# Two expert layers in a transformer kernel: where the output is multiplied by its gate row

## The chip, the cores and the metric

The kernel runs on one core of one Trainium2 chip. A core has four compute engines that matter here, each with its own instruction queue: TensorE (PE, matrix products into the accumulation memory PSUM), VectorE (DVE), ScalarE (ACT) and GpSimd (POOL). SyncE (SP) issues the transfers from device memory (DMA). The engines wait for each other through semaphores. The metric is the device time of one execution, in microseconds (us), as a median of several runs.

## The reference, cut to what matters

256 tokens of width 1024 pass through two layers (an attention or retention mixer, then an expert layer) and then through a third block that the change doesn't touch. The expert layer is:

```python
def grouped_moe(h, ...):
    combine = ...        # two experts per token, both from the token's one group of four
    for e in range(N_EXPERTS):                                # 16 experts, 4 groups
        hidden = jax.nn.silu(t @ w_gate[e]) * (t @ w_up[e])
        out = out + combine[:, e:e + 1] * (hidden @ w_down[e])
    return out

y = grouped_moe(h, ...)
x = layer_norm(DEEPNORM_ALPHA * x + (1.0 + gate) * y, ln_g[i, 1], ln_b[i, 1])
```

`gate` is one row of 1024 numbers, the same for all tokens, so the product with (1 + gate) is one by column: it may be taken before or after the tokens are put back in their places.

## The kernel before, in words

`moe_stage` is one expert layer; it runs twice (names moe0 and moe1). Tokens are sorted by their group into 128 slots per group with 0/1 matrices (`hot`), and each group's slots pass its four experts. A branch picks this "gathered" form, or a dense one when a group has more than 128 tokens.

The weights come as a stream of 2 MB chunks, three per expert (gate, up, down), 48 per layer, into a ring of three buffers. SP fetches a chunk into a buffer when `chunk_used` says that the buffer's last chunk is done with. Products are made in split precision: each chunk is worked in four quarters (q = 0 to 3, 128x1024 each). ACT copies a quarter to its high part `w_hi` (line 1115), DVE subtracts that from the quarter to get the low part `w_lo` (line 1191), and PE takes three products with them: high by high, high by low, low by high (lines 1029 to 1031 for the gate and up chunks, line 1048 for the down chunks). There is one buffer for each of the four quarters, so that ACT may write quarter q of the next chunk only when PE is done with quarter q of this one (`q_used`), and PE may start quarter q when DVE has made its low part (`lo_done`). DVE releases the chunk after its fourth quarter.

The down products of a group's four experts add up in PSUM banks 6 and 7, a tile of 128 slots x 1024. When the last is done, the sum is taken out, split in the same manner: ACT copies it to `y_hi` (`take`, line 1138), then DVE subtracts that from PSUM to get `y_lo`, a view of `halves` (`take_low`, line 1207). In the loop over groups (three turns per layer, one for each of groups 0 to 2) this stands among the next expert's gate chunk: on ACT between its quarters 1 and 2, on DVE between its quarters 2 and 3. PE waits for `y_low` only before the next down product. The last group's sum is taken out behind all weights. The order on each engine is the order of the code; there is no scheduler.

Then PE scatters the slots back to tokens (`scatter`, line 1089, `hotT` by `y_hi` and `y_lo`, four groups) into banks 0 to 3: two tiles of 128 tokens (tt), two halves of 512 columns (dh). It does groups 0 to 2 of tt = 0 first (12 products), waits for the last `y_low`, then does group 3 of tt = 0 (two products for each half) and all of tt = 1. `norm.y_made` counts the four finished quarter tiles. DVE turns each into the normalised output (`LayerNorm.vector_half`, lines 449, 451, 452): times the gate row, plus ALPHA times x, statistics. The gate row lies in `K.mod[:, 2 * D:3 * D]`; it is made during the first group's experts (`GateRow`, semaphore `gate.taken`). `LayerNorm` is shared with the two mixers.

In the second layer the norm ends with a product with rows g and b (lines 1498 and 1500) that SP fetches late (lines 483 and 484), then a second norm and transposes.

Of the kernel before, what the change touches and what calls it, by code (L numbers as in the profile page):

```python
# [401 lines left out]
class LayerNorm:  # L402

    def __init__(self, K, scope, name, s, split=False, last=False, by_half=False):
        self.K, self.s, self.split, self.last, self.by_half = K, s, split, last, by_half
        sb = lambda n, shape: scope.enter_context(K.nc.sbuf_tensor(f"{name}_norm_{n}", shape, F32))
# [38 lines left out]
    def vector_half(self, dve, n, tt, half):  # L445

        K, c, s, cols = self.K, self.c, self.s, slice(half * 512, (half + 1) * 512)
        dve.wait_ge(self.y_made, n + 1)
        c.do(dve.tensor_tensor(s[:, tt, cols], K.bank[:, 2 * (1 - half) + tt if self.by_half else 2 * tt + half, :], K.mod[:, 2 * D + half * 512:2 * D + (half + 1) * 512],
                               ALU.mult))  # L450
        c.do(dve.scalar_tensor_tensor(s[:, tt, cols], K.x[:, tt, cols], ALPHA, s[:, tt, cols], ALU.mult, ALU.add))
        c.do(dve.bn_stats(self.stats[:, tt, half, :], s[:, tt, cols]))
# [368 lines left out]
def moe_stage(K, layer):  # L821
# [15 lines left out]
    with ExitStack() as stage:  # L837
# [12 lines left out]
        g_row, b_row = K.mod[:, D:2 * D], sb("b_row", [P, D])[:]  # L850
        norm = LayerNorm(K, stage, name, room[:, 2 * D:4 * D].rearrange("p (t d) -> p t d", t=TT), split=(layer == 0), last=(layer == 1))
        gate = GateRow(K, name, 2 * layer + 1, 2)
# [97 lines left out]
        def combine(dve, c):  # L950
# [13 lines left out]

        made, spread_w, slot_taken, hot_ready, wide_ready, gathered, slots_h, slots_l, y_low = (
            s_(s) for s in ("made", "spread_w", "slot_taken", "hot_ready", "wide", "gathered", "slots_h", "slots_l", "y_low"))
        hi_done, lo_done, q_used, turned, hid_h, hid_l, taken = (
# [138 lines left out]
        def scalar_gathered(act):  # L1106
# [26 lines left out]

            def take(g, done):

                act.wait_ge(q_used, done)
                out = y_hi[:, g, :] if isinstance(g, int) else y_hi[:, bass.ds(g, 1), :].rearrange("p o d -> p (o d)")
                act.activation(out, K.bank[:, 6:8, :].rearrange("p b c -> p (b c)"), ACT.Copy).then_inc(taken, 1)
# [10 lines left out]
            def experts(i):  # L1149
                for r in range(PER_GROUP):  # L1150
# [5 lines left out]
                    elif r == 1 and i is not None:  # L1156
                        high(of(i, r, 0), {1: lambda: take(i, Q * 3 * PER_GROUP * i + Q * (3 * PER_GROUP + 3))})
                    elif r == 2 and i is None:
# [18 lines left out]
            high((LAST_DOWN, 0, None), {1: lambda: hidden_high(EXPERTS)})  # L1177
            take(GROUPS - 1, Q * (LAST_DOWN + 2))

        def vector_gathered(dve, c_):  # L1180
# [54 lines left out]
            def experts(i):  # L1235
                for r in range(PER_GROUP):
# [101 lines left out]
        def vector_dense(dve, c):  # L1338
# [24 lines left out]
            with dve.Fori(0, LOOPS) as i:  # L1363
                for r in range(2):
                    make_hidden(2 * i + (2 + r), r, 6 * i + (n0 + 7 + 3 * r))

        with nc.Block() as block:
# [2092 lines left out]
```

## Time and profile before

| | us |
|---|---|
| runs before: median of 3 (lowest, highest) | 2244.33 (2239.88, 2246.12) |
| the profiled execution, its device time | 2244.5 |
| its span, first to last instruction | 2242.8 |
| PE busy | 2077.7 (93%) |
| DVE busy | 1610.0 (72%) |
| ACT busy | 1131.2 (50%) |

All durations below come from the profiled execution. What lies around its span is 2244.5 - 2242.8 = 1.7 us. The expert layers' products by group run from about 240 to 525 us and from about 820 to 1105 us. In a view in order of time a row is an instruction or several merged; the number in brackets is the idle time of the engine before it, and after the arrow stands who ended it. A busy PE instruction is longer than the distance to the next, since they overlap: the distance counts.

### The profile page before, as it was taken

The page shows a single profiled execution, that of the slowest core. Times are in us where ns is not written, and L with a number is a line of the kernel's source. Part 1 is how long each engine was busy: PE and PEld are TensorE (multiplying, and loading weights), DVE is VectorE, ACT ScalarE, POOL GpSimd, SP SyncE. Part 2 cuts the span into 40 slices and gives each one's busy share as a digit, 9 for nine tenths or more (in the row PEclk, how much of TensorE's full clock was granted, in tenths as well). Part 3 has the DMA queues.
Part 4 walks back from the last instruction along what each step waited for, and adds up shares of the span by engine and source line. Part 5 has one row for each costly group of instructions (what it writes and reads, how often), then busy time and mean ns, then how long its engine had stood idle before and what let it go on. Part 6 is the DMA issues. An engine that isn't in the chain of part 4 may idle for free. (4 is left out here: it accounts for less than half of the span.)

```text
span 2242.8 us, 33580 instructions
## 1 busy us (share of the span) xinstructions
PE 2077.7 (93%) x11164; PEld 1720.3 (77%) x11164; DVE 1610.0 (72%) x2587; ACT 1131.2 (50%) x1641; POOL 693.7 (31%) x468
## 2 busy tenths in 40 slices
PE   5898999996999889999888999899899999999998
PEld 4775767775877776777676656899899999888887
DVE  4367888887367888888878651399779998555555
ACT  5352767774335376777550233355444444445454
POOL 6620040001757504000030004599967773000000
PEclk8997999998999989999989999999999999999999
DMA  9864789995457658899832333255444445555554
GB/s 394 310 219 148 298 305 354 343 347 193 178 201 294 246 189 322 339 347 343 306 100 75 111 109 146 88 174 174 163 136 145 141 140 180 193 188 191 191 189 150
DMA packets 76634, 485.70 MB, mean 217 GB/s; under 512 B 9472, under 2 KB 9984, under 8 KB 58624
## 3 DMA queue, kind: packets, MB, share of 16 engines
q1 hardware_dynamic: 75824, 482.88, 59.2%
q10 hardware_dynamic: 720, 1.61, 0.2%
q8 instruction: 57, 0.93, 0.2%
q14 instruction: 33, 0.27, 0.0%
HBM read 483.41 MB, written 1.05 MB: 216 GB/s over the span
## 5 line engine op out<-in xcount | busy, mean ns | idle before, releaser
L1191 DVE TENSOR_TENSOR moe_w_lo<-ring,moe_w_hi 128x1024 fp32r<-128x1024 f32 x384 | 467.1, 1252 | 52.1 <-ACT moe_w_hi L1115 38.3
L1115 ACT ACTIVATE moe_w_hi<-ring 128x1024 fp32r<-128x1024 f32 x376 | 385.1, 1058 | 75.0 <-PE bank L1048 43.2
L3083 POOL TENSOR_TENSOR peer_u_lo<-peer_u,peer_u_hi 128x512 fp32r<-128x512 f32 x253 | 343.3, 1368 | 97.0 <-ACT peer_u_hi L3108 95.0
L3023 PE MATMUL bank<-peer_hn_hi,peer_u_hi 128*128 128x256 f32 x1024 | 295.7, 289 | 17.9 <-POOL peer_u_lo L3083 11.9
L3024 PE MATMUL bank<-peer_hn_lo,peer_u_hi 128*128 128x256 f32 x1024 | 287.6, 281 | 0.0
L3025 PE MATMUL bank<-peer_hn_hi,peer_u_lo 128*128 128x256 f32 x1024 | 287.4, 281 | 0.0
L229 POOL TENSOR_TENSOR ret_all_w_lo<-ring,ret_all_w_hi 128x1024 fp32r<-128x1024 f32 x64 | 158.1, 2479 | 293.7 <-ACT ret_all_w_hi L219 293.1
L3108 ACT ACTIVATE peer_u_hi<-peer_u 128x512 fp32r<-128x512 f32 x253 | 159.2, 629 | 129.7 <-PE bank L3025 120.4
L1029 PE MATMUL bank<-moe_w_hi,moe_slots_hi 128*128 128x512 f32 x512 | 210.5, 411 | 11.7 <-DVE moe_w_lo L1191 7.7
L3023 PEld LDWEIGHTS bank<-peer_hn_hi,peer_u_hi 128*128 128x128 f32 x1024 | 194.7, 190 | 19.9 <-POOL peer_u_lo L3083 13.6
L1031 PE MATMUL bank<-moe_w_hi,moe_slots_lo 128*128 128x512 f32 x512 | 201.0, 393 | 0.0
L1030 PE MATMUL bank<-moe_w_lo,moe_slots_hi 128*128 128x512 f32 x512 | 200.6, 392 | 0.0
L3024 PEld LDWEIGHTS bank<-peer_hn_lo,peer_u_hi 128*128 128x128 f32 x1024 | 194.7, 190 | 0.0
L3025 PEld LDWEIGHTS bank<-peer_hn_hi,peer_u_lo 128*128 128x128 f32 x1024 | 194.2, 190 | 0.0
L3236 DVE TENSOR_TENSOR peer_v_lo<-peer_scores,peer_v_hi 128x1024 fp32r<-128x1024 f32 x86 | 105.4, 1225 | 102.0 <-ACT peer_v_hi L3128 102.0
L3128 ACT ACTIVATE peer_v_hi<-peer_scores 128x1024 fp32r<-128x1024 f32 x86 | 91.2, 1061 | 118.7 <-PE bank L3063 112.0
L1029 PEld LDWEIGHTS bank<-moe_w_hi,moe_slots_hi 128*128 128x128 f32 x512 | 96.0, 188 | 57.5 <-DVE moe_w_lo L1191 38.9
L3216 DVE TENSOR_SCALAR peer_scores<-consts,peer_selT 128x128 f32<-128x128 f32 x256 | 131.2, 572 | 0.0
L3063 PE MATMUL bank<-peer_hn_hi,peer_hn_lo 128*128 128x512 f32 x504 | 121.4, 390 | 0.0
L219 ACT ACTIVATE ret_all_w_hi<-ring 128x1024 fp32r<-128x1024 f32 x64 | 67.3, 1058 | 105.0 <-PE bank L258 76.4
L329 DVE CUSTOM_DVE_ANT_0 mod<-sb_mod_ring,bank 128x1024 bf16<-128x1024 f32 x64 | 77.1, 1218 | 58.6 <-DMA sb_mod_ring<-in_ada_t 40.6
L1031 PEld LDWEIGHTS bank<-moe_w_hi,moe_slots_lo 128*128 128x128 f32 x512 | 96.1, 188 | 21.8
(517 smaller groups left out, 4570.4 us busy)
## 6 DMA issues: line engine op xcount, KB each, us to landing
ring<-in_stream SPq DMA_DIRECT2D x135, 2048.0 KB, 8.3
peer_u<-in_peer_u SPq DMA_DIRECT2D x128, 512.0 KB, 3.2
peer_scores<-in_peer_v SPq DMA_DIRECT2D x86, 512.0 KB, 4.3
sb_mod_ring<-in_ada_t SPq DMA_DIRECT2D x64, 512.0 KB, 6.4
peer_u<-in_peer_v SPq DMA_DIRECT2D x42, 512.0 KB, 4.3
ret_mod_ring<-in_ada_t SPq DMA_DIRECT2D x32, 512.0 KB, 5.0
s_bz<-in_b_channel SPq DMA_DIRECT2D x4, 512.0 KB, 5.8
ring<-in_stream SPq DMA_DIRECT2D x2, 1024.0 KB, 5.0
```

The lines of the kernel that those rows point to most:

```text
L229: pool.tensor_tensor(self.shaped(self.w_lo, q, by_columns), self.quarter(n, q, by_columns), self.shaped(self.w_hi, q, by_columns).bitcast( ...
L1029: pe.matmul(K.bank[:, m, :], x_high, high[:, cols], start=(k == 0), stop=False)
L1030: pe.matmul(K.bank[:, m, :], x_high, low[:, cols], start=False, stop=False)
L1031: last = pe.matmul(K.bank[:, m, :], x_low, high[:, cols], start=False, stop=(k == KD - 1))
L1115: act.activation(w_hi[:, q, :], K.ring[:, at % RING, q * CHUNK // Q:(q + 1) * CHUNK // Q], ACT.Copy).then_inc(hi_done, 1)
L1191: dve.tensor_tensor(w_lo[:, q, :], K.ring[:, at % RING, q * CHUNK // Q:(q + 1) * CHUNK // Q], w_hi[:, q, :].bitcast(F32), ALU.subtract).th ...
L3023: pe.matmul(out, u_hi[:, b, k2, :], h_hi[:, k, :], start=(k == 0), stop=False)
L3024: pe.matmul(out, u_hi[:, b, k2, :], h_lo[:, k, :], start=False, stop=False)
L3025: last = pe.matmul(out, u_lo[:, b, k2, :], h_hi[:, k, :], start=False, stop=(k == KD - 1))
L3083: pool.tensor_tensor(u_lo[:, b, :, :], u[:, i, KD // 2 * half:KD // 2 * (half + 1), :], u_hi[:, b, :, :].bitcast(F32), ALU.subtract).then_ ...
L3108: act.activation(u_hi[:, b, :, :], u[:, i, KD // 2 * half:KD // 2 * (half + 1), :], ACT.Copy).then_inc(hi_made, 1)
L3216: last = dve.tensor_scalar(a_hot[:, b, q, :], K.iota, selT[:, 0, one], selT[:, 1, one], ALU.is_equal, ALU.mult)
```

## The change

The product with the gate row is moved from behind the scatter to in front of the split. In the two expert layers `vector_half` no longer does line 449: its first instruction is now the one with ALPHA, which reads PSUM itself. In its place DVE multiplies each group's sum in PSUM banks 6 and 7 by the row, in place (`gate_y`), and ACT's `take` waits for that (`y_gated`) and no longer for PE's last quarter. The mixers' norms stay as they were. The dense form gets the product too, at its end.

```diff
@@ class LayerNorm, vector_half
         dve.wait_ge(self.y_made, n + 1)
-        c.do(dve.tensor_tensor(s[:, tt, cols], K.bank[:, ...], K.mod[:, 2 * D + half * 512:2 * D + (half + 1) * 512],
-                               ALU.mult))
-        c.do(dve.scalar_tensor_tensor(s[:, tt, cols], K.x[:, tt, cols], ALPHA, s[:, tt, cols], ALU.mult, ALU.add))
+        y = K.bank[:, ...]
+        if not self.gated:
+            c.do(dve.tensor_tensor(s[:, tt, cols], y, K.mod[:, 2 * D + half * 512:2 * D + (half + 1) * 512], ALU.mult))
+            y = s[:, tt, cols]
+        c.do(dve.scalar_tensor_tensor(s[:, tt, cols], K.x[:, tt, cols], ALPHA, y, ALU.mult, ALU.add))
         c.do(dve.bn_stats(self.stats[:, tt, half, :], s[:, tt, cols]))
@@ moe_stage, ACT
-            def take(g, done):
-                act.wait_ge(q_used, done)
+            def take(g):
+                act.wait_ge(y_gated, g + 1)
@@ moe_stage, DVE
+            gate_row = K.mod[:, 2 * D:3 * D]
+            def gate_y(done):
+                dve.wait_ge(gate.taken, 2)
+                dve.wait_ge(q_used, done)
+                y = K.bank[:, 6:8, :].rearrange("p b c -> p (b c)")
+                dve.tensor_tensor(y, y, gate_row, ALU.mult).then_inc(y_gated, 1)
@@ in the loop over groups, DVE
-                        low(chunk(i, r, 0), {2: lambda: take_low(i)})
+                        low(chunk(i, r, 0), {0: lambda: gate_y(Q * 3 * PER_GROUP * i + Q * (3 * PER_GROUP + 3)), 2: lambda: take_low(i)})
@@ behind all weights, DVE
             low((LAST_DOWN, 0), {1: lambda: hidden_low(EXPERTS)})
+            gate_y(Q * (LAST_DOWN + 2))
             take_low(GROUPS - 1)
```

On DVE, in the loop over groups, at the gate chunk that follows a group's last down product. Before (`moe_w_lo<-ring` are the quarters' low parts, `halves<-bank` is `take_low`):

```order
L1191 TENSOR_TENSOR moe_w_lo<-ring,moe_w_hi 128x1024 [waits moe0_hi]
L1190 REGISTER_ALU
L1191 TENSOR_TENSOR moe_w_lo<-ring,moe_w_hi 128x1024 [waits moe0_hi]
L1190 REGISTER_ALU
L1191 TENSOR_TENSOR moe_w_lo<-ring,moe_w_hi 128x1024 [waits moe0_hi]
L1204 REGISTER_ALU
L1207 ISA [waits moe0_taken]
L1207 TENSOR_TENSOR halves<-bank,moe_y_hi 128x1024
L1190 REGISTER_ALU
L1191 TENSOR_TENSOR moe_w_lo<-ring,moe_w_hi 128x1024 [waits moe0_hi]
```

The same place now:

```order
L1193 TENSOR_TENSOR moe_w_lo<-ring,moe_w_hi 128x1024 [waits moe0_hi]
L1209 ISA [waits moe0_gate_taken]
L1211 TENSOR_TENSOR bank<-bank,mod 128x1024 [waits moe0_q_used]
L1192 REGISTER_ALU
L1193 TENSOR_TENSOR moe_w_lo<-ring,moe_w_hi 128x1024 [waits moe0_hi]
L1192 REGISTER_ALU
L1193 TENSOR_TENSOR moe_w_lo<-ring,moe_w_hi 128x1024 [waits moe0_hi]
L1214 REGISTER_ALU
L1217 ISA [waits moe0_taken]
L1217 TENSOR_TENSOR halves<-bank,moe_y_hi 128x1024
L1192 REGISTER_ALU
L1193 TENSOR_TENSOR moe_w_lo<-ring,moe_w_hi 128x1024 [waits moe0_hi]
```

One 128x1024 product from PSUM to PSUM stands between quarter 0 and quarter 1; quarters 1 to 3 and `take_low` are behind it.

On DVE behind the first layer's scatter, the first two quarter tiles. Before:

```order
L449 TENSOR_TENSOR moe_room<-bank,mod 128x512 [waits moe0_gate_taken,moe0_norm_y_made,moe0_x_made,moe0_norm_dve]
L451 SCALAR_TENSOR_TENSOR moe_room<-x,moe_room 128x512 [waits moe0_norm_dve]
L452 BN_STATS moe_norm_stats<-moe_room 128x6 [waits moe0_norm_dve]
L449 TENSOR_TENSOR moe_room<-bank,mod 128x512 [waits moe0_norm_y_made,moe0_norm_dve]
L451 SCALAR_TENSOR_TENSOR moe_room<-x,moe_room 128x512 [waits moe0_norm_dve]
L452 BN_STATS moe_norm_stats<-moe_room 128x6 [waits moe0_norm_dve]
L455 BN_AGGR moe_norm_mv<-moe_norm_stats 128x2 [waits moe0_norm_dve]
```

Now:

```order
L453 SCALAR_TENSOR_TENSOR moe_room<-x,bank 128x512 [waits moe0_gate_taken,moe0_norm_y_made,moe0_x_made,moe0_norm_dve]
L454 BN_STATS moe_norm_stats<-moe_room 128x6 [waits moe0_norm_dve]
L453 SCALAR_TENSOR_TENSOR moe_room<-x,bank 128x512 [waits moe0_norm_y_made,moe0_norm_dve]
L454 BN_STATS moe_norm_stats<-moe_room 128x6 [waits moe0_norm_dve]
L457 BN_AGGR moe_norm_mv<-moe_norm_stats 128x2 [waits moe0_norm_dve]
```

Two instructions for a quarter tile are left of three.

## Rows read from the trace of the kernel before

**Rows 1.** The page: the span.

```profile
span 2242.8 us, 33580 instructions
```

**Rows 2.** Windows, two turns of the group loop: stretch, length, engines' busy time, clock, DMA share, GB/s.

```profile
303.57:376.41 72.84, 70.49 (x301) 53.22 (x300) 64.26 (x58) 53.61 (x57) 9.15 (x6) 1.00 0.90 338
376.41:449.20 72.79, 70.68 (x306) 54.25 (x305) 62.95 (x58) 53.36 (x57) 0.00 (x0) 1.00 0.91 346
```

**Rows 3.** Waits, 252 to 525 us: who for whom, total us, times, longest.

```profile
ACT moe_w_hi L1115 <- DMA ring<-in_stream: 4.7, 4, 1.6
...
PE bank L1029 <- DVE moe_w_lo L1191: 3.9, 6, 0.7
```

**Rows 4.** In order of time, DVE around a group's take: start, length, what.

```profile
388.12 2.36 DVE L1191 TENSOR_TENSOR moe_w_lo<-ring,moe_w_hi 128x1024 fp32r<-128x1024 f32 x2 [0.22 <-ACT moe_w_hi L1115]
391.98 1.23 DVE L1191 TENSOR_TENSOR moe_w_lo<-ring,moe_w_hi 128x1024 fp32r<-128x1024 f32 x1 [1.51 <-ACT moe_w_hi L1115]
393.13 1.22 DVE L1207 TENSOR_TENSOR halves<-bank,moe_y_hi 128x1024 f32 x1
394.26 1.22 DVE L1191 TENSOR_TENSOR moe_w_lo<-ring,moe_w_hi 128x1024 fp32r<-128x1024 f32 x1
```

**Rows 5.** In order of time, ACT at the same place.

```profile
389.98 1.03 ACT L1138 ACTIVATE moe_y_hi<-bank 128x1024 f32 x1 [1.93 <-PE bank L1048]
390.91 3.88 ACT L1115 ACTIVATE moe_w_hi<-ring 128x1024 fp32r<-128x1024 f32 x4
```

**Rows 6.** In order of time, PE there: quarters 0, 1, 2, 3 begin.

```profile
389.69 0.39 PE L1029 MATMUL bank<-moe_w_hi,moe_slots_hi 128*128 128x512 f32 x1
...
391.05 0.39 PE L1029 MATMUL bank<-moe_w_hi,moe_slots_hi 128*128 128x512 f32 x1
...
393.26 0.50 PE L1029 MATMUL bank<-moe_w_hi,moe_slots_hi 128*128 128x512 f32 x1 [0.70 <-DVE moe_w_lo L1191]
...
395.53 0.50 PE L1029 MATMUL bank<-moe_w_hi,moe_slots_hi 128*128 128x512 f32 x1 [0.59 <-DVE moe_w_lo L1191]
```

**Rows 7.** One line: line 1207, all eight, minimum, median and maximum ns.

```profile
L1207 DVE TENSOR_TENSOR halves<-bank,moe_y_hi x8: 1217/1218/1226, 320.3 to 1106.5; 128x1024 f32 x6, 128x1024 fp32r<-128x1024 f32 x2
```

**Rows 8.** One line: ACT copies from PSUM into PSUM and into SBUF, ns.

```profile
L3101 ACT ACTIVATE bank<-bank x65: 368/368/368, 1646.7 to 1882.6; 128x256 f32<-128x256 f32 x65
L3101 ACT ACTIVATE H<-bank x63: 383/385/388, 1446.7 to 1636.6; 128x256 f32 x60, 128x256 f32<-128x256 f32 x3
```

**Rows 9.** In order of time, first layer's end: ACT, then PE, then DVE.

```profile
525.17 1.02 ACT L1138 ACTIVATE moe_y_hi<-bank 128x1024 fp32r<-128x1024 f32 x1 [4.65 <-PE bank L1048]
...
527.73 0.40 PE L1089 MATMUL bank<-moe_y_hi,moe_hotT 128*128 128x512 f32 x1
...
526.23 1.22 DVE L1207 TENSOR_TENSOR halves<-bank,moe_y_hi 128x1024 fp32r<-128x1024 f32 x1 [4.27 <-ACT moe_y_hi L1138]
...
527.86 0.17 DVE L339 TENSOR_TENSOR cols<-cols,mods 128x8 f32<-128x8 f32 x1
528.49 0.69 DVE L449 TENSOR_TENSOR moe_room<-bank,mod 128x512 f32<-128x512 f32 x1 [0.47 <-PE bank L1089]
529.22 0.69 DVE L451 SCALAR_TENSOR_TENSOR moe_room<-x,moe_room 128x512 f32<-128x512 f32 x1
```

**Rows 10.** In order of time, second layer's end: DVE, then SP.

```profile
1108.78 0.69 DVE L449 TENSOR_TENSOR moe_room<-bank,mod 128x512 f32<-128x512 f32 x1 [1.03 <-PE bank L1089]
...
1117.70 0.12 DVE L1497 RECIPROCAL moe_norm_std<-moe_norm_std 128x1 f32<-128x1 f32 x1
...
1103.63 1.04 SPq L484 DMA_DIRECT2D moe_b_row<-in_ln_b  x1
```

**Rows 11.** One line: line 484 between 1100 and 1110 us, issue to landing.

```profile
DMA to landing us min/median/max: 11.9/11.9/11.9
```

**Rows 12.** Windows, columns as in rows 2: before the first layer's end, and the stretch after it.

```profile
515.00:525.00 10.00, 8.59 (x41) 6.88 (x40) 6.02 (x6) 3.24 (x4) 0.00 (x0) 1.00 0.93 341
...
547.00:556.00 9.00, 3.37 (x16) 3.37 (x17) 4.52 (x6) 5.18 (x5) 5.78 (x3) 0.51 0.58 207
```

More of the change, by code:

```diff
@@ L402, with __init__ @@
 class LayerNorm:
-    def __init__(self, K, scope, name, s, split=False, last=False, by_half=False):
-        self.K, self.s, self.split, self.last, self.by_half = K, s, split, last, by_half
+    def __init__(self, K, scope, name, s, split=False, last=False, by_half=False, gated=False):
+        self.K, self.s, self.split, self.last, self.by_half, self.gated = K, s, split, last, by_half, gated
         sb = lambda n, shape: scope.enter_context(K.nc.sbuf_tensor(f"{name}_norm_{n}", shape, F32))
@@ L448, in vector_half @@
         dve.wait_ge(self.y_made, n + 1)
-        c.do(dve.tensor_tensor(s[:, tt, cols], K.bank[:, 2 * (1 - half) + tt if self.by_half else 2 * tt + half, :], K.mod[:, 2 * D + half * 512:2 * D + (half + 1) * 512],
-                               ALU.mult))
-        c.do(dve.scalar_tensor_tensor(s[:, tt, cols], K.x[:, tt, cols], ALPHA, s[:, tt, cols], ALU.mult, ALU.add))
+        y = K.bank[:, 2 * (1 - half) + tt if self.by_half else 2 * tt + half, :]
+        if not self.gated:
+            c.do(dve.tensor_tensor(s[:, tt, cols], y, K.mod[:, 2 * D + half * 512:2 * D + (half + 1) * 512], ALU.mult))
+            y = s[:, tt, cols]
+        c.do(dve.scalar_tensor_tensor(s[:, tt, cols], K.x[:, tt, cols], ALPHA, y, ALU.mult, ALU.add))
         c.do(dve.bn_stats(self.stats[:, tt, half, :], s[:, tt, cols]))
@@ L850, in moe_stage @@
         g_row, b_row = K.mod[:, D:2 * D], sb("b_row", [P, D])[:]
-        norm = LayerNorm(K, stage, name, room[:, 2 * D:4 * D].rearrange("p (t d) -> p t d", t=TT), split=(layer == 0), last=(layer == 1))
+        norm = LayerNorm(K, stage, name, room[:, 2 * D:4 * D].rearrange("p (t d) -> p t d", t=TT), split=(layer == 0), last=(layer == 1), gated=True)
         gate = GateRow(K, name, 2 * layer + 1, 2)
@@ L957, in combine @@
             dve.sem_inc(weights_ready, 1)
-        made, spread_w, slot_taken, hot_ready, wide_ready, gathered, slots_h, slots_l, y_low = (
-            s_(s) for s in ("made", "spread_w", "slot_taken", "hot_ready", "wide", "gathered", "slots_h", "slots_l", "y_low"))
+        made, spread_w, slot_taken, hot_ready, wide_ready, gathered, slots_h, slots_l, y_gated, y_low = (
+            s_(s) for s in ("made", "spread_w", "slot_taken", "hot_ready", "wide", "gathered", "slots_h", "slots_l", "y_gated", "y_low"))
         hi_done, lo_done, q_used, turned, hid_h, hid_l, taken = (
@@ L1156, in experts @@
                     elif r == 1 and i is not None:
-                        high(of(i, r, 0), {1: lambda: take(i, Q * 3 * PER_GROUP * i + Q * (3 * PER_GROUP + 3))})
+                        high(of(i, r, 0), {1: lambda: take(i)})
                     elif r == 2 and i is None:
@@ L1177, in scalar_gathered @@
             high((LAST_DOWN, 0, None), {1: lambda: hidden_high(EXPERTS)})
-            take(GROUPS - 1, Q * (LAST_DOWN + 2))
+            take(GROUPS - 1)
         def vector_gathered(dve, c_):
@@ L1365, in vector_dense @@
                     make_hidden(2 * i + (2 + r), r, 6 * i + (n0 + 7 + 3 * r))
+            dve.wait_ge(gate.taken, 2)
+            dve.wait_ge(norm.y_made, 2 * TT)
+            for tt in range(TT):
+                y = K.bank[:, 2 * tt:2 * tt + 2, :].rearrange("p b c -> p (b c)")
+                c.do(dve.tensor_tensor(y, y, K.mod[:, 2 * D:3 * D], ALU.mult))
         with nc.Block() as block:
```

## The prediction

> **What bounds the kernel now.** I read the two expert layers alone, since nothing else is edited, inside a span of 2242.8 us [rows 1]. First the windows: two turns of the group loop take 72.84 and 72.79 us, PE is busy for 70.49 and 70.68 of them, DVE for 64.26 and 62.95, ACT for 53, and the DMA share is 0.90 [rows 2]. PE bounds the loop, and DVE is close behind it. The waits then say what keeps PE from being quite full: it waits for DVE's low parts, and ACT waits for weights only 4 times in 273 us, 4.7 us together [rows 3]. A delay of PE in this loop is therefore not taken back by a transfer that would have been late anyway.
>
> The order of time around a group's take shows where PE waits. The chain there is serial over two engines. ACT takes the sum at 389.98, which it had waited for (1.93 us), and makes the high part of quarter 2 only then, from 390.91 [rows 5]. DVE had made quarters 0 and 1 from 388.12, idled 1.51 us, made low part 2 at 391.98, `take_low` at 393.13, low part 3 at 394.26 [rows 4]. PE begins its quarters at 389.69, 391.05, 393.26 and 395.53, and idles 0.70 and 0.59 before the last two [rows 6]. So `take`, high part 2, low part 2, `take_low`, low part 3, quarter 3 is a chain without slack that ends on PE. Whatever starts `take` later moves PE's quarter 3 by the same amount.
>
> At a layer's end PE is done with the weights, and the bound passes from PE to DVE: from 528.49 DVE works through the quarter tiles nearly without a gap, one instruction each 0.73 us (528.49 to 529.22) [rows 9].
>
> **Part 1: the product in the loop, six times.** DVE does low part 0 (388.12 and some 1.2 us, done at 389.35) and then stands before `gate_y` until PE has finished the down products, which is what ACT waited for until 389.98. Queued behind this wait are low parts 1 to 3 and `take_low`. The price of the product itself no row shows, as no DVE instruction of this trace writes PSUM. The nearest row is line 1207, which reads the same PSUM tile and an SBUF tile of the same size: 1218 ns at the median of eight [rows 7]. On ACT a copy from PSUM into PSUM takes 368 ns and one into SBUF 385 [rows 8], so a PSUM target has no price there. I take 1.22. The lower bound is the same row, since the elements are as many; the upper one is twice it, 2.44, if reading and writing PSUM took turns.
>
> `gate_y` then ends at 389.98 + 1.22 = 391.20. From DVE to the next engine a wait takes 0.05 us (low part 2 ends at 393.21, PE starts at 393.26) [rows 4, 6], so `take` starts at 391.25, 1.27 late. High part 2, low part 2, `take_low` and low part 3 follow at their old distances, and PE's quarter 3 goes from 395.53 to 396.80: +1.27. Low part 1 lies elsewhere: DVE starts it 1.14 behind `gate_y`, at 391.12, it is done at 392.35, and PE starts quarter 1 at 392.40 in place of 391.05. That is a new wait of 1.35 us on PE, but it isn't added: quarter 1 takes some 1.4 us, PE is free at 393.8, and low part 2 lets it go on at 394.53 only, which is the old 393.26 + 1.27. DVE's old idle time of 1.51 us is used up by the product, and that is the cover it has; the cover on the chain through ACT is none.
>
> From quarter 3 on all engines are late by the same 1.27, the release of the chunk and so the next fetch too. So nothing downstream changes its spacing, and nothing pays back: PE is busy for 97% of the turn. 3 turns in 2 layers: 6 x 1.27 = **+7.6 us**.
>
> **Part 2: the layer's end, twice.** ACT's take at 525.17 becomes `gate_y`; it, `take` and `take_low` stand in a row, so `take_low`, which ended at 526.23 + 1.22 = 527.45, ends 1.27 later, at 528.72. PE meanwhile scatters groups 0 to 2 until 527.73 [rows 9], 0.28 us beyond the old end: of the 1.27 the scatter hides 0.28 less the 0.05 of the wait, and group 3 starts at 528.77, 1.04 late. DVE's first quarter tile goes from 528.49 to 529.53. The small instructions of `norm_columns` (the last at 527.86 [rows 9]) shift behind `take_low` and end before that. The second layer has the same places (first tile at 1108.78 after a wait of 1.03 [rows 10]): +1.04 as well.
>
> **Part 3: the four products taken away, in each layer.** Each is one step of DVE's chain, 0.73 us [rows 9]: 4 x 0.73 = 2.9 us. PE feeds this chain early enough, also when 1.04 late: eight products of 0.23 for each later quarter tile, while DVE needs 1.45 for a tile and does statistics and transposes between. The new first instruction reads PSUM where it read SBUF; line 449 with its PSUM source and line 451 from SBUF both take 0.69 [rows 9], so I add nothing. Net of a layer's end: 1.04 - 2.92 = -1.88, twice **-3.8 us**.
>
> The page on the VectorE of the Trainium skill speaks against this last zero ("VectorE: DVE Perf Modes", section "The TRN2 errata — SBUF-src ops pay a fixed extra latency per instruction"): its table gives a PSUM source a fixed part of 120 cycles where SBUF has 58, so by an estimate from that page the instruction would grow by 0.065 us, eight times, +0.5 us in all, and the sum would be 2248.8. The trace has the two sources equal, 0.69 each, and I go by it.
>
> One cover is thin. In the second layer DVE needs row b before 1117.70 (line 1497 stands behind that wait); it is issued at 1103.63 and lands 11.9 us later, at 1115.5 [rows 10, 11]. The issue hangs on the weights and doesn't move against them, the need comes 1.88 earlier, at 1115.8. It still fits, by 0.3 us. Late by more, it would eat from the gain, at most 1.88 of it.
>
> **The sum.** 2244.5 + 7.6 - 3.8 = **2248.3 us**, 3.8 above the profiled execution, which is 0.2 above the median of the runs. It is +0.2%. A measurement of this kernel tells about 0.3% from no change, so the bounds of "the same" are 2237.6 and 2251.1.
>
> **Rivals.**
> 1. *The loop hides the product.* DVE idles 1.51 us just there [rows 4], more than the 1.22 it costs, and the DMA share of 0.90 could make the transfers the true bound, which would then not feel a late PE. Against it: the idle time lies behind `take`, not beside it, and transfers were waited for 4 times only [rows 3]. Then only the ends count: 2244.5 - 3.8 = 2240.7. Chance 0.10.
> 2. *PSUM to PSUM takes turns.* 2.44 us for the product, so 1.22 more at eight places, all on a chain: 2248.3 + 9.8 = 2258.1, slower. It decides from (2251.1 - 2248.3) / 8 = 0.35 us above my price, at 1.57 for one product. ACT's rows speak against it [rows 8]. Chance 0.08.
> 3. *The ring loses its slack.* A chunk released late is fetched late, and transfers that ran beside each other before might no longer. If each turn waited once more for weights by the mean of those seen, 4.7 / 4 = 1.2 [rows 3], that is 6 x 1.2 = 7.2 more: 2255.5, slower. Against it: release and need move together. Chance 0.12.
> 4. *The clock.* PE's new wait of 1.35 us stands in the loop. Before the first layer's end a window with 1.41 us of idle PE has a granted clock of 1.00 (2.4 GHz), and behind the layer it is 0.51 (1.2 GHz) with PE busy for 3.37 us [rows 12]. The first says that the loop keeps its clock. The second says that the next stage begins at the low level, and where the level changes may now fall otherwise against the work: half of 3.37 either way, twice, 2244.9 to 2251.7. Chance 0.10.
>
> That the change doesn't do what it says needs the dense form to run; line 1207 belongs to the other form and ran eight times [rows 7], so I give that nothing.
>
> **The numbers.** My forecast has 0.60; its own spread is some 3 us, as the runs before lie 6 apart. Within 0.3%: 0.50 of the forecast, 0.08 of rival 1, 0.02 of rival 3, 0.08 of rival 4: 0.68. Slower: 0.10, all of rival 2, 0.10 and 0.01: 0.29. Faster: 0.03. The range goes from 2240.0, just below rival 1, to 2254.5, most of the way to rival 3; outside lie rival 2, half of rival 3 and the tails, some 0.2.
>
> **What would show it.** Eight rows of the product at 1.2 us each; anything above 1.57 is rival 2. Turns of the loop of 74.1 us in place of 72.8 (72.8 again: rival 1; 75 and more with longer waits of ACT for the ring: rival 3). In a turn, PE waits three times behind the take, the first time for 1.3 us at quarter 1. From the layer's last weight product to the last instruction of the norm 1.9 us less, twice. The forecast is wrong if the turn grows by something other than 1.27, or if the ends give less than 3.8 since row b comes late.

## The result and the profile after

The changed kernel takes 2248.6 us, the median of 20 runs (2246.87 to 2252.94); the kernel before, run beside it on the same chips, takes 2244.3 (20 runs, 2239.88 to 2246.85). The ratio is 1.0023, 95% interval 1.0017 to 1.0030: slower by 4.3 us. Forecast were 2248.3 us and +3.8. Of the chances given, "within 0.3%" came true. The profiled execution has a span of 2247.9 us, 5.1 above [rows 1].

The first rows to look for are those of the new instruction. One line of the trace of the changed kernel, with count, minimum, median and maximum in ns (it answers to rows 7):

```profile
L1211 DVE TENSOR_TENSOR bank<-bank,mod x8: 1231/1232/1233, 317.4 to 1114.5; 128x1024 f32<-128x1024 f32 x8
```

A product that reads a PSUM tile and writes it back costs 1.23 us, 14 ns more than the split's subtraction from the same tile into SBUF. Next the turns of the group loop, as windows of the changed kernel (columns as in rows 2), the two turns of the first layer:

```profile
318.80:392.94 74.14, 71.04 (x304) 54.15 (x304) 64.14 (x59) 53.38 (x58) 0.00 (x0) 1.00 0.90 340
392.94:466.92 73.98, 70.96 (x304) 54.14 (x304) 64.14 (x59) 53.49 (x57) 0.00 (x0) 1.00 0.90 341
```

A turn is here taken from one ACT take to the next; cut in the same way, the turns before are 72.86 and 72.77 us in the first layer and 72.85 and 72.84 in the second. After, they are 74.14, 73.98, 74.06 and 74.11: 1.25 us longer at the mean. PE's clock is 1.00 (2.4 GHz) in both and the DMA share 0.90 beside 0.90 and 0.91 [rows 2], so neither explains it. The order of time around a group's take does. DVE of the changed kernel, then ACT, then PE (start, length, engine, what, and in brackets the wait ahead of it), where rows 4, 5 and 6 stand for before:

```profile
389.79 1.23 DVE L1193 TENSOR_TENSOR moe_w_lo<-ring,moe_w_hi 128x1024 fp32r<-128x1024 f32 x1 [0.23 <-ACT moe_w_hi L1117]
391.58 1.23 DVE L1211 TENSOR_TENSOR bank<-bank,mod 128x1024 f32<-128x1024 f32 x1 [0.56 <-PE bank L1050]
392.72 1.22 DVE L1193 TENSOR_TENSOR moe_w_lo<-ring,moe_w_hi 128x1024 fp32r<-128x1024 f32 x1
394.94 1.22 DVE L1193 TENSOR_TENSOR moe_w_lo<-ring,moe_w_hi 128x1024 fp32r<-128x1024 f32 x1 [1.00 <-ACT moe_w_hi L1117]
396.08 1.22 DVE L1217 TENSOR_TENSOR halves<-bank,moe_y_hi 128x1024 f32 x1
```

```profile
392.94 1.02 ACT L1140 ACTIVATE moe_y_hi<-bank 128x1024 f32 x1 [3.23 <-DVE bank L1211]
393.86 3.90 ACT L1117 ACTIVATE moe_w_hi<-ring 128x1024 fp32r<-128x1024 f32 x4
```

```profile
391.38 0.39 PE L1031 MATMUL bank<-moe_w_hi,moe_slots_hi 128*128 128x512 f32 x1
...
393.99 0.50 PE L1031 MATMUL bank<-moe_w_hi,moe_slots_hi 128*128 128x512 f32 x1 [1.09 <-DVE moe_w_lo L1193]
...
396.22 0.50 PE L1031 MATMUL bank<-moe_w_hi,moe_slots_hi 128*128 128x512 f32 x1 [0.57 <-DVE moe_w_lo L1193]
...
398.49 0.49 PE L1031 MATMUL bank<-moe_w_hi,moe_slots_hi 128*128 128x512 f32 x1 [0.61 <-DVE moe_w_lo L1193]
```

ACT now waits for the product (3.23 us in place of 1.93) and takes the sum 1.36 after the product began. PE's four quarters begin at 391.38, 393.99, 396.22 and 398.49. From quarter 0 to quarter 3 that is 7.11 us, where it was 5.84 [rows 6]: +1.27. It has three waits where it had two; the new one, 1.09 at quarter 1, widens the first step from 1.36 to 2.61, and quarter 2 then waits no longer than before.

The other half of the change is at a layer's end. The first layer of the changed kernel in order of time, DVE, ACT and PE (answers to rows 9):

```profile
529.41 1.23 DVE L1211 TENSOR_TENSOR bank<-bank,mod 128x1024 f32<-128x1024 f32 x1 [3.29 <-PE bank L1050]
530.68 1.02 ACT L1140 ACTIVATE moe_y_hi<-bank 128x1024 fp32r<-128x1024 f32 x1 [6.00 <-DVE bank L1211]
531.74 1.23 DVE L1217 TENSOR_TENSOR halves<-bank,moe_y_hi 128x1024 fp32r<-128x1024 f32 x1 [1.09 <-ACT moe_y_hi L1140]
...
533.02 0.51 PE L1091 MATMUL bank<-moe_y_hi,moe_hotT 128*128 128x512 f32 x1 [0.97 <-DVE halves L1217]
...
533.90 0.69 DVE L453 SCALAR_TENSOR_TENSOR moe_room<-x,bank 128x512 f32<-128x512 f32 x1 [0.37 <-PE bank L1091]
534.63 0.69 DVE L454 BATCH_NORM_STATS2 moe_norm_stats<-moe_room 128x6 f32<-128x512 f32 x1
```

Product, take and low part stand in a row, PE waits 0.97 us for them ahead of group 3, and each quarter tile of the norm has one 0.69 us instruction where it had two. The one that is left, line 453, now reads PSUM and still takes 0.69.

**The account.** I cut both traces at three events of each layer: its first low part, the start of its scatter, and the end of DVE's last instruction of its norm. What is between the two layers' expert work I call the mixer stretch, and the rest is what comes before and behind. In us, the profiled executions:

| segment | before | after | difference | forecast |
|---|---|---|---|---|
| first layer, loop | 305.87 | 310.47 | +4.60 | +3.8 |
| first layer, end | 22.73 | 21.05 | -1.68 | -1.88 |
| mixer stretch | 251.3 | 253.4 | +2.2 | 0 |
| second layer, loop | 306.28 | 310.22 | +3.94 | +3.8 |
| second layer, end | 21.08 | 19.75 | -1.33 | -1.88 |
| start and rest | 1335.5 | 1333.0 | -2.6 | 0 |

The last line is -0.4 ahead of the first layer and -2.1 behind the second. The edited segments alone sum to +5.5. The 2.2 and the -2.1 that cancel lie in code that the change does not touch; the last part of the experiments is about them.

### The profile page after: what moved, and what is told of

The parts are those of the page before. It is cut to its first block and busy times, and to the rows that moved or that the text cites. A ratio compares the mean times of both kernels' runs of the same rounds, so it can differ in the third digit from the quotient of the medians.

```text
span 2247.9 us, 33588 instructions
## 1 busy us (share of the span) xinstructions
PE 2080.6 (93%) x11164; PEld 1720.6 (77%) x11164; DVE 1607.6 (72%) x2587; ACT 1131.4 (50%) x1641; POOL 694.1 (31%) x468
## 5 line engine op out<-in xcount | busy, mean ns | idle before, releaser
L3039 PE MATMUL bank<-peer_hn_hi,peer_u_hi 128*128 128x256 f32 x1024 | 295.4, 288 | 17.9 <-POOL peer_u_lo L3099 11.9
```

The lines of the kernel that those rows point to most:

```text
L3039: pe.matmul(out, u_hi[:, b, k2, :], h_hi[:, k, :], start=(k == 0), stop=False)
```

## The experiments

The questions: is it the chain through the take that makes the loop longer, as forecast, or DVE's added work or the transfers? Do the ends give what was priced? And, once the chain was found, can it be taken off? Each of these kernels was run beside before on the same chip, and its ratio is to that. A trace shows one execution of a kernel, a median several, so the two need not agree to the microsecond.

**One half of the change at a time.** `norm_only` leaves the product out at both places, and so out of both layers:

```
-                        low(chunk(i, r, 0), {0: lambda: gate_y(...), 2: lambda: take_low(i)})
+                        low(chunk(i, r, 0), {2: lambda: take_low(i)})
...
-            gate_y(Q * (LAST_DOWN + 2))
```

> This kernel leaves the product with the gate row out of both expert layers altogether: the four products per layer behind the scatter are gone and none stands in the loop or in front of the last split. It measures part 3 alone. By the forecast's term 8 x 0.73 = 5.8 us less than before, 2238.5. The rival, that the forecast came out right because two wrong terms cancelled (the ends give less, the loop costs less), expects 2240 to 2243 here, since a shorter norm would then meet another wait, such as PE's scatter or the late row b of the second layer.

Measured: 2237.4 us beside 2245.0, ratio 0.9965 (0.9951 to 0.9978), so -7.7 where -5.8 was expected. Its loop turns are as before (72.75, 72.75, 72.79, 72.78). Its first end is 2.94 us shorter than before, where 4 x 0.73 = 2.92 was forecast. Its second gives 1.58 only, and the order of time of DVE there says why:

```profile
1110.55 0.21 DVE L457 BATCH_NORM_AGGREGATE moe_norm_mv<-moe_norm_stats 128x2 f32<-128x12 f32 x1
1111.95 0.16 DVE L1512 RECIPROCAL moe_norm_std<-moe_norm_std 128x1 f32<-128x1 f32 x1 [1.20 <-DMA moe_b_row<-in_ln_b]
```

DVE waits 1.20 us for row b. This is the thin cover of the prediction's part 3: with the need 2.92 earlier in place of 1.88, it is gone. The two ends explain 4.5 us. The profiled execution is 7.3 shorter than before, and the other 2.7 are spread over all the other segments, none of them over 1.5 (mixer stretch -0.3, rest -1.5). What they are I can't say; the interval, 3 us to either side, also holds the 5.8 expected.

`loop_only` is the other half: the product in the loop for groups 0 to 2, and the norm's products kept as well, so that the gate row comes in twice for these groups. ACT takes the last group's sum as before.

```
-        norm = LayerNorm(..., last=(layer == 1), gated=True)
+        norm = LayerNorm(..., last=(layer == 1), gated=False)
...
-            gate_y(Q * (LAST_DOWN + 2))
```

> This kernel computes something else: groups 0 to 2 are multiplied by the gate row in the loop as in the changed kernel, and all tokens once more behind the scatter as before; the last group's sum is taken out as before. It measures part 1 alone. By the forecast 6 x 1.27 = 7.6 us more than before, 2252.1, with turns of 74.1 us. If wrong terms cancelled, 2247 to 2250. If the ring loses slack (rival 3), 2254 or more.

Measured: 2253.8 us beside 2245.0, ratio 1.0036 (1.0024 to 1.0048), +8.8. A turn, as a window:

```profile
319.00:393.06 74.06, 70.91 (x304) 54.16 (x304) 64.16 (x59) 53.61 (x58) 0.00 (x0) 1.00 0.90 340
```

The four turns are 74.06, 73.97, 74.10 and 74.08 long, 1.23 more than before, and the loops 3.56 and 3.74, together 7.3. The ends are untouched (22.72 and 21.07 beside 22.73 and 21.08). This is the forecast's +7.6, 4% smaller. The start and rest are 2.6 us longer, which is where the median's further 1.2 could come from; 1.5 of them are the first 64 products behind the second layer, which take 17.01 us in place of 15.52.

**The chain or the work.** `after_late` has every instruction of the changed kernel; only their places in the quarter order of the same chunk are others. DVE multiplies behind low part 1 and subtracts behind low part 3, and ACT takes behind high part 3.

```
-                        high(of(i, r, 0), {1: lambda: take(i)})
+                        high(of(i, r, 0), {3: lambda: take(i)})
...
-                        low(chunk(i, r, 0), {0: lambda: gate_y(...), 2: lambda: take_low(i)})
+                        low(chunk(i, r, 0), {1: lambda: gate_y(...), 3: lambda: take_low(i)})
```

> The changed kernel with its takes later in the same chunk: DVE does the product behind low part 1 (not 0) and take_low behind low part 3 (not 2), ACT takes behind high part 3 (not 1). The same instructions, another order. Theory 1, the price comes from the serial chain take, high part 2, low part 2, take_low, low part 3: high parts 2 and 3 no longer wait for the take, PE's quarter 3 begins at 394.3 in place of 396.8 on the scale of before, some 0.5 us come back in the next chunk, so 2.0 us less per turn than the changed kernel, 12 in all: 2236. Theory 2, the price is DVE's work as such (it is nearly as loaded as PE in that chunk, and a longer list makes PE wait wherever the product stands): as the changed kernel, 2247 to 2249.

Measured: 2232.1 us, ratio 0.9941 (0.9928 to 0.9955); a repeat, `after_late_b`, gave 2229.2, ratio 0.9932 (0.9916 to 0.9948). The one had been expected at 2236, the other at 2232 to 2234: both gained more than that.

> The kernel of after_late again, unchanged, on the same chip as the two others: 2232 to 2234.

A turn of `after_late` as a window, then its DVE, ACT and PE around the take:

```profile
319.31:390.75 71.44, 70.47 (x306) 54.30 (x305) 63.78 (x59) 53.72 (x57) 0.00 (x0) 1.00 0.93 353
```

```profile
389.40 1.22 DVE L1211 TENSOR_TENSOR bank<-bank,mod 128x1024 f32<-128x1024 f32 x1
390.54 2.35 DVE L1193 TENSOR_TENSOR moe_w_lo<-ring,moe_w_hi 128x1024 fp32r<-128x1024 f32 x2
392.80 1.22 DVE L1217 TENSOR_TENSOR halves<-bank,moe_y_hi 128x1024 f32 x1
...
390.75 1.03 ACT L1140 ACTIVATE moe_y_hi<-bank 128x1024 f32 x1 [0.81 <-DVE bank L1211]
...
391.80 0.50 PE L1031 MATMUL bank<-moe_w_hi,moe_slots_hi 128*128 128x512 f32 x1 [0.22 <-DVE moe_w_lo L1193]
```

DVE's busy time in the turn is what it was in the changed kernel, 63.78 beside 64.14, and the turn is 2.70 us shorter, 1.4 shorter even than before. So DVE's added work does not make the loop longer; where the take stands does. High parts 2 and 3 no longer stand behind it, DVE does low parts 2 and 3 in one go, and PE's wait there is 0.22. The theory of the chain asked for a shorter turn and the theory of DVE's work for the same one. The two loops are 15.5 us shorter than in the changed kernel. That is more than the 7.6 of the chain, since the take's own stop in the order, which before had too (its two waits of 0.70 and 0.59 [rows 6]), went as well.

ACT's waits for the ring in the first layer of `after_late` (who for whom, total us, times, longest), where before has 4.7 in 4 [rows 3]:

```profile
ACT moe_w_hi L1117 <- DMA ring<-in_stream: 11.3, 10, 2.0
```

and the window's DMA share has gone from 0.90 to 0.93. These waits do not set the loop's length: in `after_late_b`, the same kernel, they are 3.7 us in 3, and its first loop, 302.66 us, is as long as the 302.87 of `after_late`. In the changed kernel itself they were 2.5 us in 2, so nothing there speaks for rival 3.

`before_late` puts the question to the kernel before: the same later place for `take` and `take_low`, with no gate row in the loop.

```
-                        high(of(i, r, 0), {1: lambda: take(i, ...)})
+                        high(of(i, r, 0), {3: lambda: take(i, ...)})
...
-                        low(chunk(i, r, 0), {2: lambda: take_low(i)})
+                        low(chunk(i, r, 0), {3: lambda: take_low(i)})
```

> The kernel before with its take behind high part 3 and take_low behind low part 3, no other edit. Theory 1 (chain): the two waits of PE behind a take (0.70 and 0.59 us) go, and most of what stands around them, 1.3 to 1.5 per turn: 2235.5 to 2236.7. Theory 2 (DVE's work as such): no change, 2244.

Measured: 2232.7 us, ratio 0.9940 (0.9926 to 0.9954). It gained more than expected, too (2235.5 to 2236.7).

```profile
317.70:388.67 70.97, 70.11 (x306) 54.39 (x305) 62.75 (x58) 53.60 (x58) 0.00 (x0) 1.00 0.93 355
```

Its turns are 70.97, 70.87, 70.99 and 70.97 us, 1.9 less than before. The expectation counted 1.3 to 1.5. In the first turn PE's idle time went from 2.16 us to 0.86, the two waits, and its busy time from 70.70 to 70.11: a product that follows a wait is longer (last section), and two of those are gone. That can be a part of the 0.59; the rest is open.

The difference to `after_late` (71.44, 71.35, 71.51, 71.50) is the price of the product in the loop once it is off the chain: 0.5 us a turn, in place of 1.25, 3 us for six. The whole loops differ by more, 4.1 us (3.8 with `after_late_b`); the rest stands ahead of the first take. The ends give back 3.0 us in the changed kernel, and the two medians come out alike. The gain of 0.6% is the order's, and the kernel before can have it without the change.

**The ends alone.** `end_only` has no product in the loop (the output lacks the gate row for groups 0 to 2), but has the product ahead of the last take, and the norm without its four.

```
-                high(of(i, r, 0), {1: lambda: take(i)})
+                high(of(i, r, 0), {1: lambda: take(i, Q * 3 * PER_GROUP * i + Q * (3 * PER_GROUP + 3))})
...
-                low(chunk(i, r, 0), {0: lambda: gate_y(...), 2: lambda: take_low(i)})
+                low(chunk(i, r, 0), {2: lambda: take_low(i)})
```

> This kernel leaves the gate row out for groups 0 to 2: the product stands only in front of the last group's split, and the product behind the scatter is gone as in the changed kernel. It measures parts 2 and 3 without part 1. By the forecast's terms 2 x (1.04 - 2.92) = -3.8 against before: 2240.5. In the trace DVE's first quarter tile starts 1.0 us later after the last weight product than before, and the norm ends 1.8 to 1.9 earlier. If the ends give less since row b comes late in the second layer (it did when the products were left out altogether, where DVE waited 1.2 us for it), 2241.5 and a wait of DVE for that transfer.

Measured: 2241.8 us beside 2244.4, ratio 0.9992 (0.9983 to 1.0001), -2.6 where -3.8 was expected. The interval, from -3.8 to +0.2, holds both the forecast and no change, so the ends have to be read from the trace. They are 21.05 and 19.39, each 1.68 and 1.69 shorter than before. In the second layer DVE does not wait for row b here, nor in the changed kernel, so the cover held. Both ends are 0.2 short of 1.88. Its mixer stretch is 253.3, 2.0 longer than before.

The missing 0.2 can be read off at the first end. The first tile of the norm begins 4.76 us behind the scatter's start (529.14 to 533.90), where it was 3.52 (524.97 to 528.49): +1.24, not the +1.04 of the forecast. Of it 0.07 is that DVE begins its product later behind PE's last down product than ACT began its take, and 0.12 that PE's first product after a wait takes 0.51 us and not the 0.40 that it took when it came to group 3 without waiting ([rows 9], and the row at 533.02 above).

**Can the ends give more?** `after_halves` cuts the last group's product, take and low part into halves of 512 columns, so that ACT takes the first half while DVE multiplies the second.

```
+            for h in range(2):
+                dve.tensor_tensor(K.bank[:, 6 + h, :], K.bank[:, 6 + h, :], gate_row[:, h * 512:(h + 1) * 512],
+                                  ALU.mult).then_inc(y_gated, 1)
...
+                act.wait_ge(y_gated, GROUPS + h)
...
-            pe.wait_ge(y_low, GROUPS)
             for dh in range(2):
+                pe.wait_ge(y_low, GROUPS + dh)
                 scatter(0, dh, (GROUPS - 1,))
```

> The changed kernel with the last group's product, take and take_low cut into two halves of 512 columns that overlap on DVE and ACT; PE waits for each half on its own. If the chain of three full instructions is what delays group 3's scatter by 1.04, the first half is ready before PE comes to it and the delay goes, twice: 2.1 us less than the changed kernel, 2246.4. The rival, that more and shorter instructions cost as much as they hide, expects 2248 to 2249.

Measured: 2246.5 us, ratio 1.0008 (0.9998 to 1.0017); 2246.4 was expected. The first end is 19.86, 1.19 shorter than in the changed kernel; the second 19.44, 0.31 shorter, where DVE again waits for row b, 1.2 us. The ends thus gave 1.5 of the 2.1 us expected, and that the median came out to the tenth is luck. The cover that `norm_only` used up is used up here too.

`late_halves` is that together with the later places of `after_late`, and `late_halves_b` its repeat.

> The later takes of after_late and the halves of after_halves together. If the two act in different places, their gains add: after_late was 12.9 below before, 2.1 more gives 15 below, 2229 to 2230. If the next bound is the fetch of weights or row b, less than 1 of the 2.1 arrives.

> The kernel of late_halves again, unchanged, as the other side of this comparison on the same chip: 2232 to 2234. The first runs of it and of after_late did not differ by the 2.1 us expected, though its ends were shorter in the trace by 1.2 us in the first layer. If that was the spread between chips and runs, it is now below after_late_b by 1 to 1.5 (2.1 less the wait for row b in the second layer); if the gain is given back behind the layers, the two are equal.

Measured: 2233.5 us (ratio 0.9946, 0.9933 to 0.9959) and 2233.2 (0.9941, 0.9923 to 0.9959). Expected had been 2229 to 2230 for the first: the medians do not show the two gains added. They could hardly do so, as the two runs of `after_late` lie 2.9 us apart. In the traces each gain is there in its segment (turns of 71.4, first end 19.86 and 19.85), but row b is waited for at the second end, 0.84 us in the repeat, and in `late_halves`:

```profile
1107.48 0.16 DVE L1522 RECIPROCAL moe_norm_std<-moe_norm_std 128x1 f32<-128x1 f32 x1 [1.44 <-DMA moe_b_row<-in_ln_b]
```

`spread_halves` moves `take_low` one chunk further, behind low part 3 of the up chunk.

```
-                        low(chunk(i, r, 0), {1: lambda: gate_y(...), 3: lambda: take_low(i)})
+                        low(chunk(i, r, 0), {1: lambda: gate_y(...)})
...
-                    low(chunk(i, r, 1), {1: lambda: hidden_low(e)} ...)
+                    low(chunk(i, r, 1), {1: lambda: hidden_low(e), 3: lambda: take_low(i)} ...)
```

> As late_halves, but take_low goes one chunk further, behind low part 3 of the up chunk, so that the gate chunk has four low parts and the product on DVE and the up chunk four low parts, the low part of the hidden tile and take_low. If the 0.5 us per turn that the loop of after_late is longer than that of before_late (71.4 against 70.9) is DVE's list in one chunk, it shrinks: 6 x 0.3 = 1.8 us less than late_halves. If DVE's list is full over both chunks, or PE then waits for take_low before the down product, no gain or a loss of up to 1 us per turn.

Measured: 2235.8 us, ratio 0.9966 (0.9953 to 0.9978), above `late_halves` by 2.3. Its turns are 72.2 to 72.4 us, 0.8 above those of `after_late`. DVE and PE there:

```profile
400.26 1.22 DVE L1219 TENSOR_TENSOR halves<-bank,moe_y_hi 128x1024 f32 x1
401.39 2.35 DVE L1195 TENSOR_TENSOR moe_w_lo<-ring,moe_w_hi 128x1024 fp32r<-128x1024 f32 x2
...
402.75 0.69 PE L1050 MATMUL bank<-moe_w_hi,moe_hid_hi 128*128 128x512 f32 x2 [0.70 <-DVE moe_w_lo L1195]
```

At its new place the subtraction stands in front of the low parts of the down chunk, and PE waits 0.70 us for them. Later is not better by itself.

`late_halves_rows` is `late_halves` with rows g and b of the second layer fetched on GpSimd's queue as soon as x is made, and not on SP's behind the last weights.

```
-                    sp.wait_ge(x_made, 8)
-                    affine_rows(sp, K, 2 * layer + 1, g_row, b_row, rows_in)
...
+                    pool.wait_ge(x_made, 8)
+                    affine_rows(pool, K, 2 * layer + 1, g_row, b_row, rows_late)
...
-                    dve.wait_ge(rows_in, 64)
+                    dve.wait_ge(rows_late, 32)
```

> The kernel of late_halves with the two late rows of the second layer's norm fetched on GpSimd's queue as soon as their buffers are free, some 190 us before they are needed, and not on SP's queue behind the last weights. In late_halves DVE waited 1.4 us for row b. If that wait is a real cost of shortening the norm, it goes, and the second layer's end is 1.4 us shorter than in late_halves; the median is 1 to 1.5 lower. If something else was late behind it, the wait moves to another row and the end stays as it was.

Measured: 2229.5 us, ratio 0.9931 (0.9914 to 0.9948). The wait for row b is gone and the second end is 18.14 us, against 19.72 and 19.12 in the two runs of `late_halves`, so the transfer had cost 1.0 to 1.6 us there. Against `late_halves_b` on the same chip the median is 3.7 lower, where 1 to 1.5 was expected, and it is not below that of `after_late_b` (2229.2), though both its ends are shorter, by 1.2 and 1.6. The intervals of the three overlap, so neither difference is shown by the medians.

**Where the untouched segments get their 2 us.** The mixer stretch has no edited code, and over the thirteen profiled executions it has two lengths: 250.8 to 251.3, and 252.8 to 253.4. Near its end stand the router's 32 small products. They are one row, of before and then of the changed kernel, each with a window inside it (the figure ahead of the DMA share is the granted clock):

```profile
781.65 4.30 PE L398 MATMUL bank<-router,hT 128*128 128x16 f32 x32
...
782.30:785.10 2.80, 2.80 (x25) 2.80 (x25) 0.67 (x3) 0.19 (x1) 0.00 (x0) 0.91 0.00 0
```

```profile
783.63 6.98 PE L398 MATMUL bank<-router,hT 128*128 128x16 f32 x32
...
784.90:789.70 4.80, 4.80 (x24) 4.80 (x24) 0.29 (x1) 0.00 (x0) 0.00 (x0) 0.50 0.00 0
```

The same 32 products take 4.30 us where the clock is 0.91 in the window and 6.98 where it is 0.50, the level of 1.2 GHz. In the five executions with the long stretch (after, `end_only`, `before_late`, `late_halves_rows`, `spread_halves`) the low level covers the router without a break; in the eight others it is the full one for a part of it. The list follows neither edit: after and `end_only` share the end's product, but `before_late` has nothing of the change, and `after_halves` and `after_late`, which have all of it, are short. The row is 2.7 us longer in the changed kernel and the stretch 2.2, as what lies ahead of the row is 0.5 shorter. The two kernels that were profiled twice have the short stretch both times; whether a kernel always has the same one, two executions cannot tell.

The same is seen behind the second layer, on the first 64 products of the next stage, of `after_late_b` and of `late_halves_rows`, with a window for each:

```profile
1118.89 14.05 PE L2101 MATMUL bank<-hT,ring 128*128 128x256 f32 x64 [2.02 <-PEq L113]
...
1119.00:1129.00 10.00, 10.00 (x47) 8.81 (x48) 5.87 (x18) 5.89 (x13) 5.94 (x6) 1.00 0.73 212
```

```profile
1118.52 16.91 PE L2111 MATMUL bank<-hT,ring 128*128 128x256 f32 x64 [2.04 <-PEq L113]
...
1119.00:1129.00 10.00, 10.00 (x35) 8.30 (x34) 6.19 (x20) 5.01 (x12) 5.59 (x5) 0.73 0.79 234
```

16.91 us with a clock of 0.73, against 14.05 at 1.00. These 2.9 us are as much as the two ends had won, but that the shorter ends bring them on is not shown. One kernel alone spreads by half as much: the two executions of `late_halves` take 15.74 and 17.07 us for these products. The execution of `late_halves_rows` is 5 us above its kernel's median, and its clock is also lower further on (0.97 beside 0.99 between 1200 and 1400 us). Over all that comes behind the second layer's norm, the two executions of `after_late` differ by 3.2 us.

This is the forecast's rival 4, at a size of 1 to 3 us a place where it was given 1.7, and it works for and against. In the changed kernel it takes 2.2 us at the router. Behind the second layer that kernel's first 64 products are not faster (15.74 us beside 15.52). Some 55 us further on some are: the same 16 products, of before and then of the changed kernel, with a window inside each:

```profile
1183.02 5.77 PE L2085 MATMUL bank<-hT,ring 128*128 128x256 f32 x16
...
1183.10:1188.60 5.50, 5.50 (x17) 4.47 (x16) 5.10 (x9) 0.00 (x0) 0.00 (x0) 0.61 0.00 0
```

```profile
1190.08 4.70 PE L2101 MATMUL bank<-hT,ring 128*128 128x256 f32 x16
...
1190.10:1194.60 4.50, 4.50 (x17) 3.79 (x16) 4.36 (x8) 0.00 (x0) 0.00 (x0) 0.76 0.00 0
```

The clock is 0.61 in the one and 0.76 in the other. That is 1.1 of the 2.1 us; the other 1.0 is the sum of smaller steps in both directions. Which sign an edit meets could not have been told from the trace of before. What fixes it I have not settled, and that the edit has a part in it is not shown.

## Why the prediction was right

By its own steps:

- **The price of the product.** Taken as 1.22 from line 1207, which does not write PSUM; 1.23 in all eight. Rival 2 (2.44, from 1.57 on slower) is out.
- **The chain of the loop.** The order named was `take`, high part 2, low part 2, `take_low`, low part 3, quarter 3, and +1.27 at PE. Quarter 0 to quarter 3 went from 5.84 to 7.11, +1.27, and the turns grew by 1.25. `loop_only` has the term alone: 7.3 us beside 7.6. The new wait at quarter 1 was said to be there (1.35 us) and not to count; it is there, the step widened by 1.25, and quarter 2 waits 0.57, where it waited 0.70.
- **What carries the chain.** The prediction claimed that no slack lay on it, and that 1.51 us of idle DVE there was no cover. `after_late` settles that: same work, other places, 15.5 us less in the two loops.
- **Rival 1, the loop hides the product.** False at this place, and partly true at the other: off the chain the product costs 0.5 us a turn.
- **Rival 3, the ring.** ACT waits for the ring 2.5 us in the first layer in place of 4.7, and 2.8 in the second beside 4.8. It took nothing here. `after_late` waits 11.3 us in its first layer and its repeat 3.7, with loops of the same length.
- **The ends.** Forecast -1.88 each; -1.68 and -1.69 in `end_only`, -1.68 and -1.33 in the changed kernel. The four products gave their 2.94 (in `norm_only`); the term that was mis-sized is the scatter of group 3, +1.24 at the first tile and not +1.04. The further 0.37 in the second layer has a row. DVE begins its product there 0.65 us behind the scatter's start, where it was 0.27 in the first layer:

```profile
1113.83 0.40 PE L1091 MATMUL bank<-moe_y_hi,moe_hotT 128*128 128x512 f32 x1
...
1114.48 1.23 DVE L1211 TENSOR_TENSOR bank<-bank,mod 128x1024 f32<-128x1024 f32 x1 [3.66 <-PE bank L1050]
...
1118.08 0.50 PE L1091 MATMUL bank<-moe_y_hi,moe_hotT 128*128 128x512 f32 x1 [1.32 <-DVE halves L1217]
```

  Both runs of `after_late` have it too and `end_only` has not, and why is open.
  The forecast let PE feed DVE's tiles early enough, with eight products of 0.23 us for a tile beside DVE's 1.45. Eight of them are 1.84 us, more than 1.45, so only the work between could cover them. It did: in the changed kernel DVE waits for PE's scatter only ahead of a layer's first tile.
- **The source of the norm's first instruction.** Priced at no change: line 453 takes 0.69 from PSUM, as line 451 did from SBUF. The estimate from the Trainium skill ("VectorE: DVE Perf Modes", section "The TRN2 errata — SBUF-src ops pay a fixed extra latency per instruction") had a PSUM source dearer by 0.065 us. The trace does not agree: 0.69 and 0.69.
- **Row b.** DVE did not wait for it in the changed kernel, but the cover was not the one forecast. The forecast had the row issued at a fixed place and 11.9 us on its way. In the changed kernel it is issued 1.7 us later against the scatter's start and takes 9.3 us; it lands 9.35 us behind that start and is needed at 11.12. In the thirteen traces that fetch or the one in its place takes 9.3 to 12.0 us, and in `end_only` it lands 0.07 us before it is needed. The four kernels that shorten the second layer's end further and leave the fetch where it was (`norm_only`, `after_halves`, `late_halves`, `spread_halves`) all waited, 0.4 to 1.4 us.
- **The sum.** +3.8 forecast, +4.3 measured. The nearness has some luck in it: the loop was 0.3 too high, the ends 0.4 to 0.8 too high in what they give, and in the profiled execution 2.2 us more in the mixer stretch, a matter of the clock, cancel against 2.1 less behind the second layer, half of them the clock's. The edited segments of the profiled execution alone say +5.5, 1.2 more than the loops of `loop_only` and the ends of the changed kernel would make (7.3 - 3.0 = 4.3). Of this 0.9 lies ahead of the first layer's first take, which comes 100.14 us after the loop's start, 99.28 in `loop_only` and 98.02 before. What fills it is open. The same stretch is 97.74 to 98.39 us long in `norm_only`, before and `end_only`, whose code is the same there, and 98.24 to 99.19 in the second layer, so as much can come from one execution to the next.

**The fastest versions** are `after_late` (0.9941, 0.9932), `before_late` (0.9940) and `late_halves_rows` (0.9931). All three beat both kernels, by 0.6 to 0.7% of before, and their intervals do not part them. As the least edit I would take `before_late`, two numbers in the order of the kernel before.

## What to carry to other kernels

An instruction added to a step that goes from one engine to the next and back cost its full length at the end of the chain here, though the engine that got it was idle for longer than that: ask on which side of the handover the idle time lies. Then ask whether the chain must be there. The work that stood behind the take did not depend on it, and moving the take behind that work brought the kernel 12 to 15 us below before, where the edit had cost 4. When a gain at a stage's end is seen in its segment and not in the whole, look at PE's granted clock in the first products of the next stage, and profile the same kernel a second time before the difference is put down to the edit.

## What was not expected of the hardware

- A VectorE product in place in PSUM costs 1.232 us for 128x1024 floats, beside 1.218 for a subtraction from PSUM into SBUF: the product with the PSUM target is 14 ns longer, and does not take twice the time.
- PE's first product after a wait is 0.50 to 0.51 us long where the same one without a wait is 0.39 to 0.40, both at full clock. At quarter 2 of before the first starts at 393.26 and the next at 393.61, 0.35 us later and not 0.23.
- The same 32 router products take 4.30 or 6.98 us and the same 64 of the next stage 14.05 or 16.9, by the granted clock that they meet. Between kernels whose code is the same there, that moves a profiled execution by 1 to 3 us a place, in either direction, and by 1.3 us between two executions of one kernel (`late_halves`, 15.74 and 17.07).
